# Seven block products in place of eight for the projections of a gated convolution layer

## The reference, cut to what matters

```
h = rmsnorm(x, norm_g)
proj = einsum('bsd,de->bse', h, w_in)          # 1024 x 4096 weights
b_g, c_g, xin, z = split(proj, 4)
u = c_g * xin
y = depthwise causal convolution of u, 3 taps
y = b_g * y * silu(z)
x = x + einsum('bse,ed->bsd', y, w_out)        # 1024 x 1024 weights
```

## Time and profile before

| | |
|---|---|
| time, 3 runs | 1220.79, 1221.99, 1222.37 us; median 1221.99 |
| profiled execution | span 1219.2 us from first to last instruction |
| PE busy | 1179.2 us (97%) |
| DVE, ACT, POOL busy | 683.4 (56%), 529.6 (43%), 570.2 us (47%) |
| mean granted PE clock | 0.992 |
| convolution layer on PE | up to 459.70 us, with 1920 large matmuls |

### The profile page before, as it was taken

One profiled execution on the slowest core, in us unless ns is written; L12 is line 12 of the kernel. 1 busy time (PEld: TensorE's weight loads), 2 busy tenths in 40 slices (PEclk: granted clock), 3 DMA queues, 4 the chain that ended last, 5 costly groups with the idle time before them and its releaser, 6 DMA issues.

```text
span 1219.2 us, 17525 instructions
## 1 busy us (share of the span) xinstructions
PE 1179.2 (97%) x5928; PEld 966.3 (79%) x5928; DVE 683.4 (56%) x1005; ACT 529.6 (43%) x839; POOL 570.2 (47%) x342
## 2 busy tenths in 40 slices
PE   5999999999999999899999999999999999988998
PEld 3888888888888888687887887878878788767887
DVE  7544323322324335858668677686776867876641
ACT  6311111111112122475765756757667476575510
POOL 6232222231333453466556475665656746654420
PEclk8999999999999999999999999999999999989999
DMA  6111111111111221111000110101001101002142
GB/s 207 35 52 52 52 52 52 34 52 52 46 57 70 86 88 53 39 41 35 26 29 19 35 35 16 36 18 35 18 17 35 35 18 34 18 18 70 52 152 90
DMA packets 19408, 59.76 MB, mean 49 GB/s; under 512 B 3760, under 2 KB 3760, under 8 KB 19376
## 3 DMA queue, kind: packets, MB, share of 16 engines
q1 hardware_dynamic: 19232, 59.34, 14.6%
q10 hardware_dynamic: 144, 0.00, 0.0%
HBM read 50.68 MB, written 8.65 MB: 49 GB/s over the span
## 4 chain that ended last, share of the span: by engine, by line
PE 82%; DVE 9%; issue 4%; ACT 3%; DMA 1%; ACTq 0%; POOL 0%; DVEq 0%; SPq 0%
PE ps L379 64%; PE ps L505 6%; PE ps L487 5%; PE ps L460 4%; DVE neg_max L1108 2%; DVE newton L1162 2%; DVE h_lo L972 1%; DVE newton L1158 1%; DVE newton L1160 1%; PE ps L528 1%; PE ps L467 1%; DMA x_t<-in_x 1%; DVE pt_lo L1121 1%; ACT y L900 0%; PE ps L652 0%
## 5 line engine op out<-in xcount | busy, mean ns | idle before, releaser
L379 PE MATMUL ps<-h_hi,w_hi 128*128 128x512 f32 x1160 | 473.1, 408 | 18.2 <-DVE h_lo L972 13.5
L379 PE MATMUL ps<-h_hi,w_lo 128*128 128x512 f32 x1160 | 456.5, 394 | 0.0
L379 PE MATMUL ps<-h_lo,w_hi 128*128 128x512 f32 x1160 | 454.2, 392 | 0.0
L1321 POOL TENSOR_TENSOR w_lo<-w_raw,w_hi 128x1024 fp32r<-128x1024 f32 x81 | 201.4, 2486 | 286.5 <-ACT w_hi L675 286.2
L379 PEld LDWEIGHTS ps<-h_hi,w_hi 128*128 128x128 f32 x1160 | 219.7, 189 | 59.4 <-DVE h_lo L972 9.6
L379 PEld LDWEIGHTS ps<-h_hi,w_lo 128*128 128x128 f32 x1160 | 218.9, 189 | 48.1
L379 PEld LDWEIGHTS ps<-h_lo,w_hi 128*128 128x128 f32 x1160 | 220.1, 190 | 35.6 <-issue 0.5
L675 ACT ACTIVATE w_hi<-w_raw 128x1024 fp32r<-128x1024 f32 x81 | 85.6, 1057 | 258.1 <-PE ps L379 256.2
L1368 POOL TENSOR_TENSOR p_big<-p_big,rdenom 128x1024 f32<-128x1024 f32 (+1 forms) x64 | 101.3, 1583 | 86.0 <-DVE rdenom L1116 85.9
L1121 DVE TENSOR_TENSOR pt_lo<-ps,pt_hi 128x512 fp32r<-128x512 f32 x160 | 105.6, 685 | 58.5 <-ACT pt_hi L796 57.8
L1368 POOL TENSOR_TENSOR p_small<-p_small,rdenom 128x768 f32<-128x768 f32 (+1 forms) x64 | 77.9, 1218 | 122.2 <-DVE rdenom L1116 121.2
(11 more groups left out here) (136 smaller groups left out, 1446.4 us busy)
## 6 DMA issues: line engine op xcount, KB each, us to landing
w_raw<-in_w_cin SPq DMA_DIRECT2D x32, 512.0 KB, 3.3
w_raw<-in_w_ain SPq DMA_DIRECT2D x32, 512.0 KB, 3.3
x_t<-in_x SPq DMA_DIRECT2D x8, 512.0 KB, 9.4
w_raw<-in_w_cout SPq DMA_DIRECT2D x8, 512.0 KB, 3.3
x_dram<-x_t SPq DMA_DIRECT2D x8, 512.0 KB, 2.6
w_raw<-in_w_aout SPq DMA_DIRECT2D x8, 512.0 KB, 4.3
out<-y SPq DMA_DIRECT2D x7, 512.0 KB, 6.9
qn<-x_dram SPq DMA_DIRECT2D x4, 512.0 KB, 3.5
```

Source lines behind the costliest of these rows:

```text
L379: last = mm(ps[:, bank, :], st[:, slot, k, :], mov[:, k, halves(h)], start=(k == 0 and st is w_hi and mov is mov_hi), stop=(k == end and s ...
L1321: TT(w_lo[:, slot, :, :], w_raw[:, slot, :, :], w_hi[:, slot, :, :].bitcast(F32), ALU.subtract).then_inc(s_wlo, 1)
```

## The change

Both projections of the convolution layer are computed by one level of a seven-product scheme. For one weight column pair and the two halves of features and positions, the weights are four blocks A11, A12, A21, A22 and the moving operand is four blocks B; C = A B takes seven block products of sums of blocks where it took eight of the blocks themselves. What this does to the program:

- The work is 8 steps for the input projection and 2 for the output projection (`ALL_STEPS` = 10). A step has 7 products by 2 groups `e`, and each product 4 feature tiles by 3 matmuls of 128x512: 14 products or 168 matmuls. Six bank roles are served by four banks of each group (Q, G, E, F); product 3 is added onto product 0 in bank Q after ACT or DVE has read it.
- The moving operand is seven pairs `b_hi0..6`, `b_lo0..6` of 128 x 4 x 512, made once for each layer part, from x normalised (`normed`) and from y. Blocks 2, 3, 4 and 6 are differences (`t1`, `t2`, `t3`, `t4`), formed in place in `xy`. For the splits ACT makes the high part, DVE the low part of blocks 1, 3, 4, 5, 6 and POOL that of 0 and 2.
- The weights land in `raw` (one place for each group). For each product ACT makes `a_hi` and POOL `a_lo` in a ring of 5. DVE forms the four weight sums of each step after the first (`sums`, `sum3`, `sum4`), POOL those of the first (`first_sums`).
- x is normalised before it is split: squares, sums, mean and reciprocal root of a half are complete before its blocks exist. `x_refine` ends that chain for a half.
- `xy` holds x, then y, and is overwritten by the differences; the residual x is loaded a second time from memory (16 transfers of 256 KB).
- DVE adds up the products from PSUM (`c11`, `u_p2`, `c22`, `c12`, `c21`; for the output projection with x, `x_p0` and `x_u`).
- The ten steps are written out without a loop. Feature tiles are done in the order 0, 4, 1, 5, 2, 6, 3, 7.
- The attention layer's instructions are the same; its tiles lie elsewhere in memory.

```diff
+PRODUCTS = 7
+Q, G, E, F = 0, 1, 2, 3
+BANK = (Q, G, E, Q, F, E, F)
+OPENS = (True, True, True, False, True, False, False)
+PER_STEP = 2 * PRODUCTS
+CONV_STEPS = KT
+ALL_STEPS = CONV_STEPS + 2
+RING = 5
+ORDER = [0, 4, 1, 5, 2, 6, 3, 7]
...
+            def load_raw(st, e):
+                if st:
+                    sp.wait_ge(s_alo, product(st - 1, PRODUCTS - 1, e) + 1)
+                for t in range(2):
+                    if st < CONV_STEPS:
+                        src = w_cin[4 * ORDER[st] + 2 * e + t]
+                    else:
+                        src = w_cout[out_tiles(st, e)[t]]
+                    sp.dma_start(raw[:, e, t, :, :], src).then_inc(s_raw[e], 16)
...
-            def conv_block(j, first):
...
-                        unit_part(t % 2, u, h, range(KT), h_hi, h_lo,
-                                  s_h if first and t == 0 else None, KT * h + 1, 1).then_inc(s_unit, 1)
-            conv_block(0, True)
-            with pe.Fori(1, KT) as j:
-                conv_block(j, False)
-            with pe.Fori(0, 2) as i:
-                for t in range(4):
-                    pe.wait_ge(s_wlo, N_COUT + 4 * i + t + 1)
-                    for h in range(2):
-                        u = 2 * t + h
-                        pe.wait_ge(s_evac, 8 * KT + 8 * i + u - 7)
-                        unit_part(t % 2, u, h, range(KT), y_hi, y_lo,
-                                  s_ylo if t == 0 else None, h + 1, 2).then_inc(s_unit, 1)
...
+            pe.wait_ge(s_vconst, 1)
+            for h in range(2):
+                pe.wait_ge(s_sqa, (KT - 1) * (h + 1))
+                mm(ps[:, F + 4 * h, :], mean_d[:, :], x_acc[:, h, :], start=True, stop=True).then_inc(s_xms, 1)
+            for sp in range(ALL_STEPS):
+                for p in range(PRODUCTS):
+                    for e in range(2):
+                        n, done = product(sp, p, e), 2 * sp + e
+                        pe.wait_ge(s_alo, n + 1)
...
+                        if p == 3:
+                            if sp < CONV_STEPS:
+                                pe.wait_ge(s_p0, done + 1)
+                            else:
+                                pe.wait_ge(s_q8, done + 1 - 2 * CONV_STEPS)
...
+                        if p == 5:
+                            pe.wait_ge(s_v, done + 1)
+                        if p == 6:
+                            pe.wait_ge(s_c22, done + 1)
+                        for k in range(KH):
+                            if e == 0 and sp in (0, CONV_STEPS):
+                                pe.wait_ge(s_blo[p], (KH if sp else 0) + k + 1)
+                            for st, mov in ((a_hi, b_hi[p]), (a_hi, b_lo[p]), (a_lo, b_hi[p])):
+                                last = mm(ps[:, 4 * e + BANK[p], :], st[:, n % RING, k, :], mov[:, k, :],
+                                          start=(OPENS[p] and k == 0 and st is a_hi and mov is b_hi[p]),
+                                          stop=(k == KH - 1 and st is a_lo), skip_group_check=True)
+                        last.then_inc(s_prod, 1)
...
+            def a_high(n):
+                sp, q = divmod(n, PER_STEP)
+                p, e = divmod(q, 2)
+                if p in (0, 1, 6):
+                    act.wait_ge(s_raw[e], 32 * (sp + 1))
+                elif sp == 0:
+                    act.wait_ge(s_s0, 4 * e + p - 1)
+                else:
+                    act.wait_ge(s_s, 8 * (sp - 1) + (2 * e + p - 1 if p < 4 else 4 + 2 * (p - 4) + e + 1))
+                if n >= RING:
+                    act.wait_ge(s_prod, n - RING + 1)
+                A(a_hi[:, n % RING, :, :], a_source(sp, p, e), ACT.Copy).then_inc(s_ahi, 1)
...
+            def b_high(b, k, layer):
+                if b in (2, 3, 4, 6):
+                    act.wait_ge(s_t2[(2, 3, 4, 6).index(b)], KH * layer + k + 1)
+                elif layer == 0:
+                    act.wait_ge(s_hn[(0, 1, 5).index(b)], k + 1)
+                else:
+                    act.wait_ge(s_gat, GATING * (ORDER.index(k if b == 0 else KH + k) + 1))
+                if layer:
+                    act.wait_ge(s_prod, product(CONV_STEPS - 1, b, 1) + 1)
+                elif b == 6:
+                    act.wait_ge(s_hn[2], KH)
+                A(b_hi[b][:, k, :], block_at(b, k), ACT.Copy).then_inc(s_bhi[b], 1)
...
+                    if sp == CONV_STEPS:
+                        if q == 0:
+                            b_high(1, KH - 1, 1)
+                            b_high(6, 0, 1)
+                            b_high(6, 1, 1)
+                            b_high(3, KH - 1, 1)
+                            b_high(4, KH - 1, 1)
+                            b_high(5, KH - 1, 1)
+                            b_high(6, 2, 1)
+                            b_high(6, 3, 1)
...
+            def x_sum(h, k):
...
+                if k == 1:
+                    TT(x_acc[:, h, :], x_sq[:, 0, :], x_sq[:, 1, :], ALU.add).then_inc(s_sqa, 1)
+                else:
+                    dve.wait_ge(s_sqa, (KT - 1) * h + k - 1)
+                    TT(x_acc[:, h, :], x_acc[:, h, :], x_sq[:, k % 4, :], ALU.add).then_inc(s_sqa, 1)
...
+            def x_refine(h):
+                dve.wait_ge(s_xln, 2 * h + 2)
+                own(TT(rs_t[:, h, :], x_inv[:, h, :], x_inv[:, h, :], ALU.mult))
+                own(STT(rs_t[:, h, :], ps[:, F + 4 * h, :], EPS, rs_t[:, h, :], ALU.add, ALU.mult))
+                own(STT(x_inv[:, h, :], rs_t[:, h, :], 3.0, x_inv[:, h, :], ALU.subtract, ALU.mult))
+            def normed(m, h):
+                return STT(xy[:, m, halves(h)], xy[:, m, halves(h)], g1n[:, m:m + 1], x_inv[:, h, :],
+                           ALU.mult, ALU.mult)
+            def b_low(b, k, layer):
+                dve.wait_ge(s_bhi[b], KH * layer + k + 1)
+                TT(b_lo[b][:, k, :], block_at(b, k), b_hi[b][:, k, :].bitcast(F32), ALU.subtract)\
+                    .then_inc(s_blo[b], 1)
...
+            def t1(k, layer):
+                y_ready(layer, k)
+                dve.wait_ge(s_blo[0], KH * layer + k + 1)
+                TT(xy[:, k, halves(0)], xy[:, k, halves(1)], xy[:, k, halves(0)], ALU.subtract)\
+                    .then_inc(s_t2[0], 1)
...
+            def t2(k, layer):
...
+                dve.wait_ge(s_t2[0], KH * layer + k + 1)
+                dve.wait_ge(s_blo[2], KH * layer + k + 1)
+                TT(xy[:, k, halves(0)], xy[:, KH + k, halves(1)], xy[:, k, halves(0)], ALU.subtract)\
...
+            def t3(k, layer):
...
+                TT(xy[:, k, halves(1)], xy[:, KH + k, halves(1)], xy[:, k, halves(1)], ALU.subtract)\
+                    .then_inc(s_t2[2], 1)
...
+            def t4(k, layer):
...
+                TT(xy[:, KH + k, halves(0)], xy[:, KH + k, halves(0)], xy[:, k, halves(0)], ALU.subtract)\
+                    .then_inc(s_t2[3], 1)
...
+            def sums(sp, e):
+                dve.wait_ge(s_raw[e], 32 * (sp + 1))
+                dve.wait_ge(s_alo, product(sp - 1, 3, e) + 1)
+                at = 8 * (sp - 1) + 2 * e
+                a11, a21, a22 = (raw[:, e, t, h * KH:(h + 1) * KH, :] for t, h in ((0, 0), (1, 0), (1, 1)))
+                TT(s_t[:, e, 0, :, :], a21, a22, ALU.add).then_inc(s_s, 1)
+                dve.wait_ge(s_s, at + 1)
+                TT(s_t[:, e, 1, :, :], s_t[:, e, 0, :, :], a11, ALU.subtract).then_inc(s_s, 1)
...
+            def sum3(sp, e):
+                a11, a21 = (raw[:, e, t, 0:KH, :] for t in range(2))
+                dve.wait_ge(s_s, 8 * (sp - 1) + 2 * e + 1)
+                TT(a21, a11, a21, ALU.subtract).then_inc(s_s, 1)
...
+            def c11(sp, e):
+                at = group_at(sp, e)[0]
+                dve.wait_ge(s_prod, product(sp, 1, e) + 1)
+                if sp < CONV_STEPS:
+                    dve.wait_ge(s_p0, 2 * sp + e + 1)
+                else:
+                    dve.wait_ge(s_q8, 2 * (sp - CONV_STEPS) + e + 1)
+                TT(at, ps[:, 4 * e + G, :], at, ALU.add).then_inc(s_c11, 1)
...
+            def x_p0(sp, e):
+                at, m = group_at(sp, e)[0], out_tiles(sp, e)[0]
+                dve.wait_ge(s_prod, product(sp, 0, e) + 1)
+                dve.wait_ge(s_xr[2 * m], 16)
+                TT(at, ps[:, 4 * e + Q, :], at, ALU.add).then_inc(s_q8, 1)
...
+            for sp in range(ALL_STEPS):
+                if sp >= CONV_STEPS:
+                    x_p0(sp, 0)
...
+                if sp == CONV_STEPS - 1:
+                    b_low(1, KH - 1, 1)
+                    t4(0, 1)
+                    t4(1, 1)
+                    for k in range(KH - 1):
+                        b_low(4, k, 1)
+                    t3(KH - 1, 1)
+                    t2(KH - 1, 1)
+                    b_low(3, KH - 1, 1)
+                    b_low(4, KH - 1, 1)
+                if sp + 1 < ALL_STEPS:
+                    for e in range(2):
+                        sum3(sp + 1, e)
+                    for e in range(2):
+                        sum4(sp + 1, e)
...
+            def a_low(n):
```

(19 more changed lines are left out.)

831 lines of the change are left out of this document (547 added, 284 removed).

## The result

The changed kernel is slower: 1241.1 us, median of 4 runs (1240.5 to 1242.1), against 1221.4 us of the kernel before on the same chip (1220.5 to 1222.4). The ratio is 1.0166, 95% interval 1.0152 to 1.0180. The profile's span lies 1.8 us under the time of the same execution (1240.3 for 1242.11); the 2.8 us that the forecast added came from the median of several.

What follows compares the result with a forecast made beforehand. PE was taken to bound the kernel, busy 97% of 1219.2 us. -54.8 + 37 + 24 + 10 = +16 us gave 1235.4, plus 2.8 for the median: 1238 us, range 1206 to 1262 (likeliest case 1226 to 1256).

Steps and rivals of the forecast that it cites:

- Matmuls: Both projections: seven products for eight, 192 and 48 fewer matmuls at 0.2267 and 0.2343 us, saving 54.8 us.
- Start: Up to the end of step 0: normalising and splitting on DVE delay PE, +37 us (14 to 45).
- without meetings: Lower end of each stage: no DVE instruction on two SBUF operands is held up by POOL; step 0 ends at 74 us.
- with all: Upper end at the start: DVE pays for every POOL instruction; step 0 ends at 105 us.
- Ordinary steps: Steps 1 to 6: the new work hides under PE's 38.1 us a step, cost 0, by a thin margin.
- upper sum: Steps 1 to 6: DVE's 19.8 us plus all 17.6 us of POOL's low parts, 37.4 us a step.
- Step 7 and the passage: Step 7 and the turn to the output projection: PE waits on DVE's and other queues, +24 us (13 to 36).
- The queue of 24 instructions behind the gate: Step 8: the last t4, 24th on DVE behind tile 7's gate, takes 16.6 us and delays PE's seventh product.
- The gap in step 7 at product 11: Sign expected in the new profile if the forecast was right: a PE gap in step 7 at that product.
- Step 9: End of the output projection: PE idles ahead of the forget unit, +10 us, between 6.7 and 15.
- rare meetings: Rival: POOL seldom holds DVE up, all three stages at their lower ends, 1201 us, faster; chance 0.28.

Runs made afterwards that it cites:

- e2: Changed kernel with POOL's subtractions and sums in the convolution layer each replaced by two fills that read nothing (work left out): 1205.4 us, ratio 0.9868.
- e3: Changed kernel with DVE reading the last products of the output projection (c12, c21) ahead of most h_lo: 1237.8 us, ratio 1.0132.
- e9: Changed kernel with squares summed on PE, normalising factor read from PSUM, and start, passage and last reads reordered, all together: 1212.8 us, ratio 0.9930.
- e7: Changed kernel with the squares of x summed by sixteen PE matmuls in place of fourteen DVE sums: 1233.8 us, ratio 1.0107.
- e10: e9 with four changes of order, among them the squares of half 0 summed by DVE again: 1207.3 us, ratio 0.9892.

## Why the prediction was right, and where it was off

The forecast was 1238 us and slower; the sum of its steps +16 us, the measured change of the span +21.1.

- **Matmuls, -54.8 forecast, -57.4 measured.** Wherever PE was fed without a break the pace was 0.2267 us, in the output projection too (168 in 38.08 us in step 9), where I had kept the 0.2343 of the earlier trace rows: 348.2 + 90.0 - 380.8 = 57.4. The slower matmuls behind a gap are counted with their stages. Why the 384 were slower before, evenly and without a gap, is not shown.
- **Start, +37 forecast, +40.9 measured** (100.45 against 59.6). The first matmul was put at 41 us and came at 40.2. The step that held is the one that set the two ends: 74 without meetings, seen as 74.7 in e2, and 105 with all. The forecast took 8 us off for gaps, and the kernel gave back 4.6 of them. This term was mis-sized by 3.9 us.
- **Ordinary steps, 0 forecast, 0 measured**: steps 1 to 6 took 38.08 us each. The margin was not thin: DVE was busy 191.17 of 261 us there, 27.9 us a step where the upper sum had 37.4.
- **Step 7 and the passage, +24 forecast, +27.0 measured**: 1.9 in step 7 and 25.1 in step 8. The queue of 24 instructions behind the gate was 16.6 us by forecast and 16.0 by the trace, without meetings, since POOL had nothing to do there. The forecast was 13 us without meetings and half of 22.7 for them. That half was a choice and not worked out, and it is luck that it came so near: e2 still lost 16.4 us, and the meetings account for the other 10.6. Two details were wrong. The gap in step 7 at product 11 did not come (PE's pauses in step 7 and at its end were at most 1.2 us). And the sum had no term for the weight transfer of step 8, which held DVE up for 4.0 us ahead of the gate (3.0 in e2). The transfer was issued at 362.28 us, behind POOL's last low part of step 7 for its group, which stood behind four `b_lo`, and landed 4.6 us later.
- **Step 9, +10 forecast, +10.6 measured.** The 10 was again chosen, between 6.7 and 15. e3 confirms what was said of the order: with the reads first the gap is 6.0 us.
- **Not forecast, +1.8**: the first half of the forget unit and the mean square behind it took 9.2 us for 7.4, on a PE that had idled (granted clock 0.69 in the stretch ahead of them). The rest of the program is 1.7 us shorter, within the 2.7 us by which it varies between the versions.

Of the rivals, rare meetings (1201 us) is about what e2 shows without POOL's reads, at 1205 us: its size was near, its condition false, since the two meet wherever both have a queue. The Trainium skill, "SBUF — State Buffer", section "Who interferes with whom", calls this an exclusive lock between DVE with two SBUF inputs and a reading GpSimd instruction. It also says that DVE with at most one SBUF input is free of it outside the two-port modes, and that against two SBUF inputs a GpSimd instruction which only writes does not contend. All three agree with the rows here: two inputs 1.56 us (12.46 / 8), one input 0.67 (5.36 / 8), and 0.68 beside POOL's fills. The section names `tensor_scalar` among the forms that can enter a two-port mode, and here the tap product, a TENSOR_SCALAR on one SBUF operand, did meet POOL: 0.75 us where it was not held up, 1.63 beside a low part in the changed kernel.

## What to carry to other kernels

Work saved on the bound engine has a price at the places where its feed is not yet running: count there what must be done before the first product, not the busy shares. Where DVE and POOL both have a queue and DVE takes two operands from SBUF while POOL reads it, count a pair of their instructions at nearly the sum of the two (1.67 us here, for 0.75 and 1.26), and take one operand of DVE from PSUM where it can stand there. And ahead of the last result that the next stage needs, move everything out of the queues that only the next stage needs.

## What the runs showed of the hardware that was not expected

- POOL's fills did not hold up DVE's forms on two SBUF operands, not even when three of them made POOL busy longer than its subtractions (0.684 us for `b_lo`).
- One form they did hold up: the tap product, a TENSOR_SCALAR with a single SBUF operand. Two of the eight in e2, the second of them with a fill that started at 346.76 us, took 1.14 and 1.09 us for 0.75, and the next fill took 0.95 for 0.53:

```profile
302.62 0.75 DVE L1351 TENSOR_SCALAR ca<-ubuf,taps 128x1024 f32<-128x1024 f32 x1
346.74 1.09 DVE L1351 TENSOR_SCALAR ca<-ubuf,taps 128x1024 f32<-128x1024 f32 x1
347.34 0.95 POOL L1758 MEMSET a_lo<- 128x512 f32 x1
```

- POOL pays as well: a 128x512 low part took 1.27 us beside a DVE that reads PSUM and 1.71 us beside one that reads two SBUF operands; a 1024-wide `w_lo` 2.77 us beside `h_lo`, 2.40 alone.
- A float32 product with the mean matrix at the start took 1.2 us (eight in 9.67 us, e9), more than the 0.69 us of the sum on DVE that it replaced. In e7 the exchange paid, since DVE was the bound; for half 0, where DVE was idle, e10 took it back.
